# Attention beside two projection groups instead of one, with top-k rounds, last keys and down chunks in another order

## What is computed

```python
h = rmsnorm(x); P = h @ w_in              # q f i g | q k v | q_idx k_idx w_idx
y_a = hgrn2(...)                          # gated by silu(g)
score = sum_h w_idx * relu(q_idx @ k_idx) ; sel = top_k(score, 128)
y_b = softmax(q @ k_sel * scale + bias) @ v_sel      # causal, 8 heads
x = x + rmsnorm(concat(y_a, y_b) @ w_o)
x = x + rmsnorm((silu(h2 @ w_gate) * (h2 @ w_up)) @ w_down)
```

## Time and profile before

| what | value |
|---|---|
| median of 3 runs | 706.2 us (703.04 to 706.27) |
| the profiled execution | 704.14 us, its span 702.4 us |
| PE busy | 685.9 us (98%) |
| DVE busy | 381.9 us (54%) |
| ACT busy | 259.8 us (37%) |
| POOL busy | 93.9 us (13%) |
| mean granted clock of PE | 0.997 |

### The profile page before, as it was taken

One profiled execution on the slowest core, in us unless ns is written; L12 is line 12 of the kernel. 1 busy time (PEld: TensorE's weight loads), 2 busy tenths in 40 slices (PEclk: granted clock), 3 DMA queues, 4 the chain that ended last, 5 costly groups with the idle time before them and its releaser, 6 DMA issues.

```text
span 702.4 us, 8568 instructions
## 1 busy us (share of the span) xinstructions
PE 685.9 (98%) x3472; PEld 579.0 (82%) x3472; DVE 381.9 (54%) x553; ACT 259.8 (37%) x401; POOL 93.9 (13%) x130
## 2 busy tenths in 40 slices
PE   8999999999999979999999999999999999999996
PEld 5978888888988878888988888888888888888884
DVE  3865999999668689337643343343433432212216
ACT  5656434444257377235532223133232231211213
POOL 1810220000407478002100000000000000000001
PEclk9999999999999999999999999999999999999998
DMA  8443042342521100351350332323313223233103
GB/s 261 122 150 87 35 120 61 105 159 67 181 61 60 61 1 30 152 185 55 97 170 9 115 114 68 119 75 105 120 61 119 96 85 119 64 116 112 69 0 120
DMA packets 49352, 68.59 MB, mean 98 GB/s; under 512 B 5025, under 2 KB 39841, under 8 KB 49314
## 3 DMA queue, kind: packets, MB, share of 16 engines
q1 hardware_dynamic: 44320, 60.07, 26.6%
q0 software_dynamic: 3280, 7.35, 3.0%
q10 hardware_dynamic: 1714, 0.64, 0.4%
HBM read 65.40 MB, written 4.74 MB: 100 GB/s over the span
## 4 chain that ended last, share of the span: by engine, by line
PE 81%; DVE 12%; ACT 4%; issue 3%; DMA 0%; POOL 0%; DVEq 0%; ACTq 0%
PE PS L1143 70%; PE PS L1333 2%; DVE w_lo L787 2%; DVE A L858 2%; DVE top L857 1%; DVE A L1031 1%; PE PS L1252 1%; PE PS L1215 1%; PE PS L1186 1%; PE PS L1344 1%; PE PS L1239 1%; PE PS L1192 1%; ACT A L702 1%; PE PS L1191 1%; PE PS L1276 1%
## 5 line engine op out<-in xcount | busy, mean ns | idle before, releaser
L1143 PE MATMUL PS<-hT_lo,w_hi 128*128 128x512 f32 (+2 forms) x584 | 218.3, 374 | 0.9 <-DVE w_lo L819 0.5
L1143 PE MATMUL PS<-hT_hi,w_lo 128*128 128x512 f32 (+2 forms) x584 | 217.2, 372 | 0.0
L1143 PE MATMUL PS<-hT_hi,w_hi 128*128 128x512 f32 (+2 forms) x584 | 217.2, 372 | 0.0
L787 DVE TENSOR_TENSOR w_lo<-raw,w_hi 128x2048 fp32r<-128x2048 f32 x49 | 114.5, 2336 | 176.0 <-ACT w_hi L543 175.7
L543 ACT ACTIVATE w_hi<-raw 128x2048 fp32r<-128x2048 f32 x49 | 93.8, 1914 | 210.2 <-PE PS L1143 209.5
L1143 PEld LDWEIGHTS PS<-hT_lo,w_hi 128*128 128x128 f32 (+1 forms) x584 | 109.7, 188 | 20.1 <-DVE w_lo L819 0.8
L1143 PEld LDWEIGHTS PS<-hT_hi,w_hi 128*128 128x128 f32 (+1 forms) x584 | 109.6, 188 | 19.5
L1143 PEld LDWEIGHTS PS<-hT_hi,w_lo 128*128 128x128 f32 (+1 forms) x584 | 109.7, 188 | 18.5
L1143 PE MATMUL PS<-w_hi,ff 128*128 128x512 f32 x352 | 108.2, 389 | 0.0
L1143 PEld LDWEIGHTS PS<-w_hi,ff 128*128 128x128 f32 x352 | 66.1, 188 | 13.7
L1143 PE MATMUL PS<-w_lo,ff 128*128 128x512 f32 x176 | 68.5, 389 | 0.0
(11 more groups left out here) (170 smaller groups left out, 762.3 us busy)
## 6 DMA issues: line engine op xcount, KB each, us to landing
raw<-in_w_in_dram SPq DMA_DIRECT2D x16, 1024.0 KB, 5.6
raw<-in_w_gate_dram SPq DMA_DIRECT2D x11, 1024.0 KB, 5.2
raw<-in_w_up_dram SPq DMA_DIRECT2D x11, 1024.0 KB, 5.3
raw<-in_w_down_dram SPq DMA_DIRECT2D x11, 1024.0 KB, 4.9
raw<-in_w_o_dram SPq DMA_DIRECT2D x4, 1024.0 KB, 4.9
A<-in_x_dram SPq DMA_DIRECT2D x4, 512.0 KB, 5.6
A<-in_x_dram POOLq DMA_DIRECT2D x4, 512.0 KB, 7.4
out_dram<-A SPq DMA_DIRECT2D x8, 256.0 KB, 2.0
```

The source lines that it names most:

```text
L787: dve.tensor_tensor(lo, raw_view(j), hi.bitcast(F32), ALU.subtract).then_inc(s_lo, 1)
L1143: o = pe.matmul(out, lhs[a], rhs[b], start=(first and n == 0), stop=(last and n == 2))
```

## The change

- The units go beside two groups: 0 to 3 beside group 31 (after its k = 4 to 7), 4 to 8 beside group 32 (after k = 3 to 7). The unit order has five heads of block 1 instead of three before the last two heads of block 0.
- In the groups 31 and 32 the evacuation of each head is a step of its own, and the last of the units stands between the two heads.
- Top-k rounds: one instead of two at groups 13 to 20, three instead of two at groups 22 to 25, two at the others from 21 on. They now end at group 29 instead of 27.
- The first `w_o` chunk is split whole, at group 30, and the recurrence's high and low parts are made at units 23 to 31. The steps of `y_hi_b`, `y_lo_b` and of the turning of a block come one unit later.
- The last two down chunks go block by block: both chunks' part of block 2, then both chunks' part of block 3, half by half.

```diff
-    EARLY = HEADS_B - 2
-    unit_order = [(b, h) for b in range(TB) for h in range(HEADS_B)]
-    unit_order[EARLY:EARLY + 5] = [(1, 0), (1, 1), (1, 2), (0, EARLY), (0, EARLY + 1)]
-    Y_A_AT = {12 + 2 * h: h for h in range(HEADS_A)}
-    QUARTER_AT = {22: 0, 24: 1, 26: 2, 28: 3}
+    unit_order = [(0, h) for h in range(HEADS_B - 2)] + [(1, h) for h in range(5)] + [(0, HEADS_B - 2), (0, HEADS_B - 1)]
+    unit_order += [(1, h) for h in range(5, HEADS_B)] + [(b, h) for b in range(2, TB) for h in range(HEADS_B)]
+    LAST_KEYS = unit_order.index((0, HEADS_B - 2))
+    BESIDE = {len(groups) - 2: (4, range(4)), len(groups) - 1: (3, range(4, 9))}
+    Y_A_AT = {23 + 2 * h: h for h in range(HEADS_A)}
...
             def topk_share(g):
-                if g < G_L0 - 1:
+                if g < G_L0 - 1 or G_OFF <= g <= G_YNORM:
                     return (1, 2) if last_of_chunk(g) else (2, 1)
-                return (1, 1)
+                return (1, 0) if g < G_ENDS else (1, 1)
...
-                if g + 1 == len(groups):
+                if g in BESIDE:
                     topk_rounds(48)
-                    for i in range(EARLY - 1):
+                    units = BESIDE[g][1]
+                    for i in units[:-1]:
                         attend(i)
-                evac(g)
+                    stack_lo(g, (0,))
+                    attend(units[-1])
+                    stack_lo(g, (1,))
+                else:
+                    evac(g)
...
-                if last_of_chunk(g) and j + 2 < J_WO and j + 2 != AHEAD:
+                if last_of_chunk(g) and j + 2 <= J_WO and j + 2 != AHEAD:
                     split(j + 2)
...
-                if g + 1 == len(groups):
-                    return lambda k: attend(k + EARLY - KT) if k >= KT - EARLY else None
+                if g in BESIDE:
+                    k0, units = BESIDE[g]
+                    return lambda k: attend(units[k - k0]) if 0 <= k - k0 < len(units) else None
...
+            for t in range(2):
+                row_block(J_DN + C_LAST - 1, 2 * C_LAST - 2, ff_parts, t, False, False)
+            pe.wait_ge(s_lo, J_DN + C_LAST + 1)
+            for t in range(2):
+                row_block(J_DN + C_LAST, 2 * C_LAST, ff_parts, t, False, True).then_inc(s_dn, 1)
+            row_block(J_DN + C_LAST - 1, 2 * C_LAST - 2, ff_parts, 2, False, False)
+            row_block(J_DN + C_LAST, 2 * C_LAST, ff_parts, 2, False, True).then_inc(s_dn, 1)
+            t = TB - 1
+            for half in range(2):
+                for k in range(2 * C_LAST - 2, 2 * C_LAST + 2):
```

More of the change, by code:

```diff
@@ L287, in qk_bank @@
         def qk_bank(i):
-            return 6 if i % 3 == 2 and i < unit_order.index((0, EARLY)) else QK_BANK[i % 3]
+            return 6 if i % 3 == 2 and i < LAST_KEYS else QK_BANK[i % 3]
         def ended(b):
@@ L595, in _, with evac @@
             act.dma_start(grow, g_sb).then_inc(s_grow, 16)
-            def evac(g):
+            def evac(g, heads=(0, 1)):
                 j, kind, c, m = groups[g]
@@ L611, in evac @@
                 elif kind == "ak":
-                    for e in range(2):
+                    for e in heads:
                         act.activation(KS[0:DH, 2 * h + e, :], ps[e * DH:(e + 1) * DH, :], ACT.Copy).then_inc(s_sth, 1)
@@ L704, in _ @@
                     o.then_inc(s_ss, 1)
-            for i in range(EARLY - 1, UNITS + PV_LAG):
+            for i in range(9, UNITS + PV_LAG):
                 attend(i)
@@ L914, in y_gate, with stack_lo @@
                                              scalar=gn[:, 0:1], in1=v, op0=ALU.mult, op1=ALU.mult).then_inc(s_yg, 1)
-            def stack_lo(g):
+            def stack_lo(g, heads=(0, 1)):
                 j, kind, c, m = groups[g]
@@ L921, in stack_lo @@
                 scale = -DH ** -0.5 if kind == "aq" else 1.0
-                for e in range(1 if kind == "ikw" else 2):
+                for e in heads[:1] if kind == "ikw" else heads:
                     dve.wait_ge(s_sth, before + (2 if kind == "ikw" else e + 1))
@@ L1003, in attend @@
                     y_norm_b(b)
-                b = block_done(i - 5)
+                b = block_done(i - 6)
                 if b is not None:
@@ L1362, in _ @@
                     turn_y()
-            for i in range(EARLY, UNITS + PV_LAG):
+            for i in range(9, UNITS + PV_LAG):
                 attend(i)
@@ L1430, in _, with ff_parts @@
                     feature_group(w_split(j), m, P, 2 * up + m, S // 2 if c == 0 else 0, S, s_gu)
-            for c in range(FT // 2):
+            def ff_parts(k):
+                return ff[:, k, 0, :], ff[:, k, 1, :]
+            C_LAST = FT // 2 - 1
+            for c in range(C_LAST - 1):
                 pe.wait_ge(s_lo, J_DN + c + 1)
                 pe.wait_ge(s_flo, 2 * c + 2)
-                last = c == FT // 2 - 1
                 for t in (2, 3, 0, 1) if c == 0 else range(TB):
@@ L1438, in _ @@
                         pe.wait_ge(s_fr, FT)
-                    def acts(k):
-                        return ff[:, k, 0, :], ff[:, k, 1, :]
-                    if last and t == TB - 1:
-                        w = w_split(J_DN + c)
-                        for half in range(2):
-                            for kk in range(2):
-                                o = passes(kk, [x[:, t * P:(t + 1) * P] for x in acts(2 * c + kk)],
-                                           [x[:, kk, half * 512:(half + 1) * 512] for x in w],
-                                           PS[:, 2 * t + half, :], False, kk == 1)
-                            o.then_inc(s_dn, 1)
-                        continue
-                    o = row_block(J_DN + c, 2 * c, acts, t, c == 0, last)
-                    if last:
-                        o.then_inc(s_dn, 1)
-                if not last:
-                    o.then_inc(s_rows, 1)
+                    o = row_block(J_DN + c, 2 * c, ff_parts, t, c == 0, False)
+                o.then_inc(s_rows, 1)
+            pe.wait_ge(s_flo, FT)
+            pe.wait_ge(s_lo, J_DN + C_LAST)
+            for t in range(2):
[8 more added lines that the diff above has]
+                for k in range(2 * C_LAST - 2, 2 * C_LAST + 2):
+                    w = w_split(J_DN + k // 2)
+                    o = passes(k, [x[:, t * P:(t + 1) * P] for x in ff_parts(k)],
+                               [x[:, k % 2, half * 512:(half + 1) * 512] for x in w],
+                               PS[:, 2 * t + half, :], False, k == 2 * C_LAST + 1)
+                o.then_inc(s_dn, 1)
     return nc
```

37 lines of the change are left out of this document (9 added, 28 removed).

## The result

The changed kernel takes **709.13 us** (median of 7 runs, 708.4 to 709.64), the kernel before 703.81 us on the same chip (7 runs, 703.04 to 706.27): a ratio of **1.0065 [1.0048, 1.0083]**, some 4.6 us slower. The forecast was 705.5 us and no measurable change; 709.13 lies at the upper end of the range given.

A forecast was written before the change was run, and what follows sets the result against it. TensorE, busy 98% of the span, was taken as the bound, so only its waits could change. Added 8.5 us less removed 7.1 us gave +1.4 on 704.14: 705.5 us, range 698.0 to 709.5.

The forecast's parts named there:

- Fewer rounds in the levels: Groups 13 to 20: with eight rounds gone, TensorE's waits for VectorE before the levels go, -1.5 us.
- `y_gate` later: At unit 0: four rounds ahead of `y_gate` start it 6.0 us later, so TensorE waits, +3.9 us.
- the first rival: VectorE's idle time in groups 21 to 26 absorbs the rounds, waits of 6.8 us fall away: 698.7 us, chance 0.27.
- Minimum for unit 3: At unit 3: VectorE's minimum comes late, +1.2 us, and the exponential holds the turning by another +0.3 us.
- All of group 31's keys: At unit 4, after four sets of group 32: TensorE waits for group 31's second head, +1.4 us.
- Last keys head by head: At unit 11: group 32's evacuation around unit 8 takes 3.5 us against 1.8 us of work, +1.7 us.
- Attention waits that go: In the attention: waits for copied probabilities and block divisions go, -4.7 us, or -3.3 if half of 2.7 stayed.
- Down chunks: At the tail: with block 2 complete 2.7 us earlier, VectorE's last step starts earlier, -0.9 us.
- the rival that named the clock: TensorE's clock falls to half rate in the new 3.9 us wait at unit 0: 710.5 us, chance 0.18.
- slower by over 0.5%: Outcome for the whole kernel: the clock's case together with the contended split, chance 0.20.
- the list of what would show it: Signs: over 3 us wait at unit 0, none before levels, `y_gate` about 6 us later, last step within 0.2 us.
- the second rival: The clock falls in the wait at unit 0, 710.5 us, chance 0.18; sign: granted clock below 1 in 240 to 260.

The follow-up runs named there:

- four_back: The changed kernel with a second top-k round back at groups 13, 15, 17 and 19, so the rounds end at group 27; 702.78 us, ratio to before 0.9981.
- fill_wait: The changed kernel with 36 small matmuls, results unused, in the wait for `y_gate` at unit 0; 708.41 us, ratio to before 1.0070.
- old_rounds: The changed kernel with the top-k rounds where the kernel before had them; 705.31 us, ratio to before 1.0019.
- down_only: The kernel before with only the new order of the last two down chunks; 702.82 us, ratio to before 0.9988.
- changed_fill_keys: The changed kernel with 12 small matmuls, results unused, at the wait for the last keys; 708.13 us, ratio to before 1.0051.
- rounds_only: The kernel before with only the changed kernel's top-k rounds; 704.99 us, ratio to before 0.9992.
- one_more: four_back with six heads of block 1, not five, before the last two of block 0; 704.71 us, ratio to before 1.0005.
- both_whole: four_back with groups 31 and 32 each evacuated whole and six heads of block 1 first; 701.30 us, ratio to before 0.9945.
- fill_keys: four_back with 12 small matmuls, results unused, at the wait for the last keys; 700.41 us, ratio to before 0.9948.

## Why the prediction was wrong

Point by point, in the terms of its sum:

- *Fewer rounds in the levels*, -1.5: measured -2.1 up to the turning. Right in kind, 0.6 short, and four_back shows that half of the removed rounds was enough.
- *`y_gate` later*, +3.9: measured 4.11. Right, in place, cause and size. The rounds were not absorbed, so the first rival (0.27) was out.
- *Minimum for unit 3*, +1.5: no such wait in the profile after, but 1.14 us in fill_wait, where the clock stayed up. The term was right; TensorE spent it in slow matmuls. So of the two terms, 1.2 and 0.3, nothing stands in the changed kernel's waits.
- *All of group 31's keys*, +1.4: 0.86 in the changed kernel, about 1.3 in old_rounds and four_back.
- *Last keys head by head*, +1.7: measured 0.81 + 1.32 + 0.80 = 2.9 us. The chain of ScalarE's and VectorE's steps was near right: 3.7 us from the first copy (251.25) to the end of the second low half (254.97), where the count had 3.5, and TensorE has some 2 us of work beside it, where it had 1.8. That gives the first two waits, 2.1. The count left out the third, 0.80 us for probabilities that ScalarE copies only behind an exponential (255.47), which itself waits 1.23 us for its minimum behind the second low half.
- *Attention waits that go*, -4.7: 0.5 stays, so -4.2.
- *Down chunks*, -0.9: measured -0.8, alone and in the change.

All waits between the turning and `w_o` together: 8.4 us in the changed kernel (4.11, 0.86, 0.81, 1.32, 0.80, 0.51), 4.7 before (2.00, 0.21, 1.09, 0.77, 0.59), so +3.7, where the forecast's terms give 8.5 - 4.7 = +3.8. This agreement is in part luck: the last keys were put 1.2 too low, and the minimum was put at 1.5 where no wait is left. With the levels (-2.1) and the tail (-0.8) the waits make +0.8 us, near the forecast's +1.4. But the profiled executions differ by +6.0 once the start-up is taken out (+6.7 and -0.8). **The missing 5 us are the step that failed: the sum took TensorE at full clock through the attention**, because the wait of 2.0 us "did not bring it down". That was one execution. down_only has the same wait with a fall behind it. In place of full clock the runs show two stretches at half rate. From unit 0's logits to unit 3's TensorE works for 5.0 us (237.06 to 242.07); in fill_wait, with the clock up, 3.0 us and 1.14 us of waiting: **2.0 us** more work, which take the place of waits, so that taking this fall away gains nothing. The stretch behind the last keys takes **2.8 us** more than with the clock up (35.83 against 33.07), and nothing hides that: without a gap TensorE works at 0.50 from 256.53 to 262.24, 5.7 us, in which full rate would have taken about 2.9 (an estimate that agrees). 0.8 + 2.0 + 2.8 = 5.6 of the 6.0 us; the rest of 0.4 I cannot place.

So the rival that named the clock had the right cause at the wrong place. It was tied to the wait for `y_gate`, "from the point where the wait is longer than the 2.5 us above". The fall came there indeed, and removing it gained nothing; it came again where no wait was longer than 1.32 us. The trace's end, on which that rival leaned, shows a fall with no matmul behind it, so it could not show a price. What came, +0.65%, is the case "slower by over 0.5%", which had a chance of 0.20.

Two readings in the prediction were off without moving its sum. TensorE has no wait behind 280 in the trace before, which is three fifths of the span and not a third. And the median of three runs, 706.2, was high: in seven runs on one chip it was 703.81, so the profiled execution was no low one.

The signs in the list of what would show it came out as the forecast has them: the wait at unit 0, no waits in the levels, `y_gate` tied to its rounds (it starts 4.9 us behind group 31's first matmul, and before it started 1.3 us ahead of it: 6.2 us later), the last step just behind the last root (by 0.24 us). The granted clock below 1 in 240 to 260, the sign set for the second rival, came too. The rival's time of 710.5 us was nearly measured, but by luck: it priced the fall behind `y_gate`, and the second one costs.

The prediction passed over a rule that speaks of this. What the rows show is a fall after three waits of 0.80, 1.32 and 0.90 us (four_back, ending at 247.55, 249.53 and 250.84), with small matmuls between them. The Trainium skill (TensorE: Matmul & The Clock Gate, A second HAM failure mode: psum-queue depth-cycling) says that frequent short idle spells between groups of matmuls can make the clock swing between its two levels. The trace agrees.

## What to carry to other kernels

These are lessons of this kernel's runs. Work moved "to where the engine has time" lands in front of whatever stands next in that engine's queue: ask for the first instruction behind it that the critical engine waits for, and move only as much as that one has room for (four rounds, not eight). Don't put a step that needs another engine's answer between the two halves of an evacuation. Count short waits that lie close together as a risk for the clock, and price a fall at the place where the critical engine has no slack, which need not be the longest wait; one profiled execution without a fall doesn't show that there is none.

## What was unexpected in the hardware

- The clock's fall varies from execution to execution of one kernel. The kernel before: in the comparison whose median is 703.80 its runs with a mean granted clock of 0.997 took 702.88 to 704.03 us, those of 0.994 and 0.995 took 703.80 to 707.76. The changed kernel had 0.988 to 0.990 in all seven runs, so it fell in each. A mean can mislead: one run of down_only lists 0.946 and took 704.03 us, where its others, at 0.993 to 0.998, took 702.15 to 704.30.
- A fall right after a wait was partly seen late: in four_back the waits end at 250.84 and the clock falls at about 252.2 (0.60 in the window 252 to 253). In changed_fill_keys it stayed at 1.00 through the whole wait of 4.12 us for `y_gate`, which ended at 237.54, and fell only behind it (0.82 in 238 to 239, 0.50 in the next); in the changed kernel, with the same wait, it fell in the wait (0.96 in 234 to 235, 0.50 in the next).
- The start-up has two lengths. The first projection matmul came at 16.7 to 17.4 us in ten of the fourteen profiled executions and at 18.6 to 19.2 in four (before, rounds_only, one_more, both_whole), whatever the change. It is 2 us of noise, as large as the effects sought, and counting from that matmul takes it out.
- Half rate can be free, and need not be: 275.45 us to `w_o` with the clock at 0.50 from 235 to 241 (changed) and with 1.00 there (fill_wait); but 2.8 us for the fall behind the last keys, in both.
- What was done in a wait can matter less than what follows it: in fill_keys TensorE still stood idle for 1.16 us, and the clock stayed at 1.00 with 12 unused matmuls behind that wait. In changed_fill_keys the same edit did not hold it (0.61 in 256 to 260).
